# Writing the unread result of a dot product to a bf16 scratch in a PEER retrieval kernel

## What is computed

```python
def peer_block(xb, w_q, sub_keys, expert_u, expert_v):
    tb = xb.shape[0]
    q = jnp.einsum('td,de->te', xb, w_q).reshape(tb, PEER_HEADS, 2, D_HALF)
    s = jnp.einsum('thpc,hpkc->thpk', q, sub_keys).astype(jnp.float32)
    sv, si = lax.top_k(s, PEER_TOPK)
    ...
    expert = (i1 * N_KEYS + i2).reshape(tb, PEER_HEADS * PEER_TOPK)
    g = jax.nn.softmax(cv, axis=-1).reshape(tb, PEER_HEADS * PEER_TOPK)
    act = jax.nn.gelu(jnp.einsum('tkd,td->tk', expert_u[expert], xb).astype(jnp.float32),
                      approximate=False)
    w = (g * act).astype(xb.dtype)
    return jnp.einsum('tk,tkd->td', w, expert_v[expert])
```

## Time and profile before

| | us |
|---|---|
| median of 3 runs | 3370.08 |
| lowest and highest | 3369.46, 3372.25 |
| profiled execution | 3370.17 |
| its span, first to last instruction | 3368.4 |

### The profile page before, as it was taken

How to read it: one execution, slowest core, us unless ns; L and a number is a source line. 1 busy time by engine, 2 the same in 40 slices (tenths; PEclk the granted TensorE clock), 3 DMA queues, 4 the chain that set the end, 5 groups by cost and what they waited for, 6 DMA issues and landing times.

```text
span 3368.4 us, 25767 instructions
## 1 busy us (share of the span) xinstructions
PE 1756.1 (52%) x7978; PEld 716.8 (21%) x7978; DVE 1990.1 (59%) x5165; ACT 370.3 (11%) x947; POOL 1959.8 (58%) x2091
## 2 busy tenths in 40 slices
PE   4399999234444444444444444444555455554334
PEld 4244444211111111111111111112222222221001
DVE  0221412676666666666666666667777777777542
ACT  0201201100101010101010101011111111111000
POOL 0000000367777776777677767777777777776775
PEclk7699999666766666757666767766776766766667
DMA  9600204599999999999999999999999999999998
GB/s 356 222 0 25 75 0 149 199 376 409 409 404 407 406 408 400 409 406 407 406 407 404 406 402 407 407 406 408 402 406 403 404 403 398 409 408 387 409 408 333
DMA packets 334187, 1169.72 MB, mean 347 GB/s; under 512 B 39222, under 2 KB 46150, under 8 KB 332008
## 3 DMA queue, kind: packets, MB, share of 16 engines
q0 software_dynamic: 298256, 1090.65, 81.7%
q1 hardware_dynamic: 29368, 73.60, 6.1%
q10 hardware_dynamic: 6432, 3.90, 0.4%
HBM read 1154.54 MB, written 13.48 MB: 347 GB/s over the span
## 4 chain that ended last, share of the span: by engine, by line
DMA 36%; POOL 16%; DVE 15%; issue 8%; PE 7%; ACT 0%; POOLq 0%; DVEq 0%; ACTq 0%
DMA v_rows<-in_expert_v_dram,v_idx 16%; DMA wide<-in_expert_u_dram,u_idx 11%; DMA u_rows<-in_expert_u_dram,u_idx 9%; POOL v_rows L1106 8%; PE ps_y L1494 6%; POOL wide L1094 6%; DVE u_rows L1360 4%; POOL u_rows L1094 2%; DVE wide L1360 2%; DVE pick L1313 1%; DVE pick L1319 1%; DVE pick_f L1324 1%; PE ps_a L1437 1%; DVE top_i L1278 1%; DVE top_i L1285 1%
## 5 line engine op out<-in xcount | busy, mean ns | idle before, releaser
L1494 PE MATMUL ps_y<-v_rows,spread 128*32 128x512 f32 x4032 | 837.3, 975 | 1321.3 <-DMA v_rows<-in_expert_v_dram,v_idx 1321.1
L1106 POOL DMA_INDIRECT v_rows<-in_expert_v_dram,v_idx x1008 | 954.0, 946 | 423.4 <-issue 266.8
L1360 DVE CUSTOM_DVE_ANT_0 wide<-wide,ps_x 128x1024 f32<-128x1024 f32 x512 | 617.2, 1220 | 419.2 <-DMA wide<-in_expert_u_dram,u_idx 402.7
L1360 DVE CUSTOM_DVE_ANT_0 u_rows<-u_rows,ps_x 128x1024 f32<-128x1024 f32 x512 | 614.7, 1219 | 370.4 <-DMA u_rows<-in_expert_u_dram,u_idx 367.9
L1094 POOL DMA_INDIRECT wide<-in_expert_u_dram,u_idx x512 | 486.4, 950 | 192.2 <-issue 112.9
L1094 POOL DMA_INDIRECT u_rows<-in_expert_u_dram,u_idx x512 | 481.7, 941 | 164.7 <-issue 96.4
L1494 PEld LDWEIGHTS ps_y<-v_rows,spread 128*32 128x32 f32 x4032 | 163.9, 150 | 1868.7 <-issue 1853.9
L1437 PE MATMUL ps_a<-wide,h2T 128*128 128x256 f32 x1152 | 287.3, 405 | 7.7 <-ACT h2T L1141 6.5
L1437 PEld LDWEIGHTS ps_a<-wide,h2T 128*128 128x128 f32 x1152 | 227.7, 204 | 119.4 <-issue 79.4
L624 POOL DMA_DIRECT2D wide<-in_w_q_dram x1 | 1.1, 1077 | 393.2 <-PE mix_pair L794 393.2
L794 PE MATMUL mix_pair<-hT,wide 128*128 128x512 f32 x512 | 220.8, 593 | 0.0
(11 more groups left out here) (230 smaller groups left out, 1665.5 us busy)
## 6 DMA issues: line engine op xcount, KB each, us to landing
ada_w<-in_w_ada_dram SPq DMA_DIRECT2D x12, 2048.0 KB, 14.5
v_rows<-in_expert_v_dram,v_idx POOLq DMA_INDIRECT x1008, 8.9
wide<-in_w_in_dram SPq DMA_DIRECT2D x1, 10240.0 KB, 37.0
x_in<-in_x_prompt_dram SPq DMA_DIRECT2D x16, 512.0 KB, 4.1
wide<-in_w_q_dram POOLq DMA_DIRECT2D x1, 8192.0 KB, 23.6
wide<-in_expert_u_dram,u_idx POOLq DMA_INDIRECT x512, 8.8
u_rows<-in_expert_u_dram,u_idx POOLq DMA_INDIRECT x512, 8.9
w_out<-in_w_out_dram SPq DMA_DIRECT2D x1, 4096.0 KB, 44.1
```

The costliest lines, as they stand in the source:

```text
L1106: pool.indirect_dma_start(home[:, :], None, t["expert_v"][0], bass.IndirectOffsetOnAxis(ap=idx, axis=0)).then_inc(landed, 16)
L1360: dve.tensor_tensor_reduce(rows[:, :], rows[:, :], x, 1.0, 0.0, ALU.mult, ALU.add, acc).then_inc(done, 1)
L1494: last = pe.matmul(ps_y[32 * j:32 * j + 32, c * HALF:(c + 1) * HALF], spread[n % 2][:, 32 * m:32 * m + 32], homes[j][0][:, c * HALF:(c + 1 ...
```

## The change

The elementwise result of each product goes into one of two bf16 tensors of 128 x 1024, `u_junk0` and `u_junk1` in turn, and no longer over the rows. The inputs, the sum and the increment of `dots_done` stay as they are. Since product g writes the scratch of product g - 2, it gets a wait until that one is done.

```diff
         y_junk = sb("y_junk", [P, D], BF16)
+        u_junk = [sb(f"u_junk{i}", [P, D], BF16) for i in range(2)]
         gate2_b = sb("gate2_b", [P, D])
...
                 rows = u_rows[g % RING]
                 dve.wait_ge(u_landed[g % RING], 16 * (g // RING) + 16)
-                dve.tensor_tensor_reduce(rows[:, :], rows[:, :], x, 1.0, 0.0, ALU.mult, ALU.add, acc).then_inc(done, 1)
+                if g >= 2:
+                    dve.wait_ge(dots_done, min(g - 1, WIDE * ROUNDS))
+                if g >= WIDE * ROUNDS + 2:
+                    dve.wait_ge(sample_dots, g - 1 - WIDE * ROUNDS)
+                dve.tensor_tensor_reduce(u_junk[g % 2][:, :], rows[:, :], x, 1.0, 0.0, ALU.mult, ALU.add, acc).then_inc(done, 1)
```

## The result

The changed kernel takes 3375.96 us (median of 15 runs, 3372.80 to 3379.82) against 3370.08 us for the kernel before (15 runs, 3367.51 to 3372.25): ratio 1.0019, 95% interval 1.0011 to 1.0026. It is slower, by 5.9 us. The time lies within the predicted range of 3364 to 3377 us, but the forecast was no change and the interval excludes that. Ratios are of fast runs; the one slow run in what follows, of wait_loop_dve at 3719.9 us, is left out of its ratio.

The account below looks back on a forecast made before the run. The prediction took the DMA engines to set the end after 740 us, with VectorE the bound only at the start. Its terms summed as 0 + 0 + 0 on 3370.17 us, forecast 3370 us, range 3364 to 3377 us.

Parts of the forecast that it names:

- What bounds the kernel: From 740 to 3200 us the DMA engines, at 405 GB/s, now and then the V ring; VectorE only at the start.
- The product: VectorE's 1024 products over U and 8 for the samples stay at 1.22 us with a bf16 result; term 0.
- The wait on VectorE: 924 more bare waits ahead of products, conditions met about 1.07 us early; taken as 0, upper end +9.8 us.
- the MAX8's row: A search's MAX8 with a bare wait ahead starts 1.14 us after the product before it; grounds for pricing waits at 0.
- Instruction fetch: 924 more VectorE instructions, 0.04 MB of code, 0.1 us at 405 GB/s; left out of the sum.
- Writes to SBUF: VectorE writes 2 KB per partition and product in place of 4 KB; taken as 0, bound 24 us.
- the ring: Slots for gathered U rows are freed at the same moment as before, since GpSimd still waits for the dot.
- a bf16 product holds GpSimd up: Gathers beside VectorE's ordinary products lengthen, 0.22 us a product; 82 us slower, 3452 us, chance 0.03.
- a shorter product: Products at 0.61 us, half their time, shorten the VectorE-bound start by 14 us; 3356 us, chance 0.03.
- fewer writes: Fewer SBUF writes by VectorE free the DMA engines; 24 us faster at most, 3346 us, chance 0.02.
- the wait costs the overlap: Back-to-back products on VectorE start 1.30 us apart, not 1.15; 5.0 us, 3375 us, with the rounds' share 3380; chance 0.06.
- The signs: Profile checks: product 1220 ns, spacing 1.15 us, gathers 937 ns, 405 GB/s, start waits near 7.1 and 7.5 us.

Follow-up runs that it names:

- wait_loop_dve: Kernel before plus a 16-turn VectorE loop behind each round's weights: 1024 more bare waits run, 192 instructions more of code; 3373.73 us, 1.0015.
- bf16_in_place: Kernel before with the product's result written as bf16 over the first half of the rows, no scratch, no added wait; 3370.23 us, 1.0001.
- the bursts: Kernel before plus bare waits in a row on VectorE behind each round's weights: 32 a round 3377.47 us, 1.0023; 64 a round 3384.11 us, 1.0043.
- wait_pe: Kernel before plus four bare waits on TensorE after each group of V matmuls, 1024 in all; 3370.16 us, 1.0002.
- skip_spread: Kernel before with VectorE jumping over 24 never-run bare waits ahead of every fourth product, 6708 instructions more of code; 3408.97 us, 1.0116.
- scratch7_no_wait: Kernel before with seven bf16 scratch tensors in turn, every eighth product in place, no added waits; 3369.87 us, 1.0000.
- wait_spread2: Kernel before plus two bare waits, on a semaphore complete long ago, ahead of each product on VectorE, 2064 more instructions; 3381.72 us, 1.0036.
- skip_small: Kernel before with VectorE jumping over one bare wait ahead of every fourth product, 774 instructions more of code; 3375.73 us, 1.0017.

## Why the prediction was wrong

**What bounds the kernel** held, and more firmly than I used it. The DMA engines set the end after 740 us. So a wait that lies within VectorE's 1.07 us of slack didn't count, and what takes from the gathers' rate did.

**The product** held: 0 predicted, 1221 ns measured where the earlier trace rows has 1221, bf16_in_place at 1.0001. The Trainium skill (VectorE: DVE Perf Modes, "What auto-detection actually checks") was right against the halved write. For the sample products, both inputs of which lie in SBUF, the row went from 1224 to 1226 ns.

**The wait on VectorE** held too. It was taken at 0 by the MAX8's row, and the spacing stayed at 1.14 us; the waits at the start came out at 6.18 and 7.53 us where the earlier trace rows has 7.11 and 7.54. A wait isn't free when nothing covers it, 96 ns in the bursts; here the product ahead covers it. That each VectorE instruction goes through the full dispatch, a wait too (the Trainium skill, Vector Engine (DVE) Microarchitecture Reference, "Instruction fetch and dispatch"), is borne out by the bursts and had no say in the change.

**Instruction fetch is the step that failed**: "that is 0.04 MB, 0.1 us at 405 GB/s. I leave it out." It was priced by bytes, and from the wrong row: q8 is TensorE's queue (wait_pe moved it, the change left it at 60 packets), and VectorE's code comes over q14. The amount was about right all the same (0.06 MB, seven packets); the unit was wrong. By the skipped blocks a packet of VectorE's code costs 0.72 us beside the gathers, and more gather packets run slow with it; seven make 5.0 us, against 5.9 measured. The term was too small by a factor of some 50, and a bound from above for it, which every other term had, was missing. The Trainium skill has a page on this that I didn't weigh (Runtime: NRT & Kernel Launch, "Instruction fetch mechanics"). It says that code streams in through a DMA queue of the engine's own and calls the cost of a block boundary mostly hidden. On VectorE it was hidden here; on the gathers it was not. That fetching runs straight on, as the Trainium skill has it there, agrees with skip_spread, where code that was jumped over was fetched all the same.

**Writes to SBUF** at 0 held (scratch7_no_wait at 1.0000), and so did the ring: the rival in which a bf16 product holds GpSimd up didn't occur, since the gathers' median (939 against 937 ns) and the waits in the earlier trace rows came back nearly unchanged. The two rivals on the faster side, a shorter product and fewer writes, fall with bf16_in_place and scratch7_no_wait.

**The rival "the wait costs the overlap"** named 3375 us and the time came out at 3376. Its mechanism is refuted: the overlap is there, and wait_spread2 with two waits for each product still starts one every 1.15 us. The right time was luck. It is luck too that the time lies in the range, whose upper end was set by this rival.

**The signs** let me down in one place. I would have called the prediction wrong at a DMA rate moved by more than 2 GB/s. In a stage of 2460 us at 405 GB/s one GB/s is 6 us, which is the whole effect. In the same way I took 0.2%, 6.7 us, as the least that a measurement can tell; the interval of 1.0011 to 1.0026 tells 0.1%.

## What to carry to other kernels

Where gathers keep the DMA engines busy all the time, as here, an instruction added to VectorE isn't free just because VectorE is idle. Count the added instructions and divide by 128; in this kernel each such packet amid the gathers cost 0.7 to 1 us. For another kernel that is an estimate to be tried. Choose between a buffer and a wait with that in mind, since here a seven-fold scratch without waits cost nothing and a two-fold one with waits cost 6 us. And give a small term its upper bound in the unit in which it could hurt, before it is left out.

## What the runs showed of the hardware

- VectorE's instructions are fetched 128 at a time in packets of 8 KB (2048 more instructions, 16 packets more), TensorE's in packets of 16 KB (four more for 1024).
- A VectorE packet amid the gathers costs 0.72 us of the span (skip_spread against skip_small); for a ScalarE packet no cost could be told. Sixteen of ScalarE's came out at 1.2 us, interval -2.0 to 4.0, where VectorE's price makes 11.5. Why the two differ is open. No run told whether it is how the packet reaches the engine, or where the code lies in memory.
- Slow gather packets are thickest 16 to 28 us behind the fetch in the kernel before (15 to 26 ns of excess per us against a mean of 9) and 8 to 24 us behind it in the changed kernel (12 to 22 against 11), with a smaller hump in the first four microseconds. That lag was seen and not explained, and the packets' added time is a good half of the loss and not the whole.
- Instructions that are jumped over are fetched: 6708 skipped or jumping instructions brought 53 packets.
- A met bare wait on VectorE costs 96 ns when 64 stand in a row, and nothing that can be seen when it lies under a running product.
- By the same price the kernel before pays too. Its trace has 37 VectorE packets behind 640 us, by the time they take; 37 x 0.72 is an estimate of 27 us, if each costs what an added one does. A VectorE program with its rounds in a loop might get some of that back. It wasn't tried, and no kernel here beat the one before.
